# Rows of 320 instead of 272 columns for the operands of the feed-forward matmuls

## The reference

```python
D_FF = 2816

def rms_norm(x, gain):
    x32 = x.astype(jnp.float32)
    y = x32 * lax.rsqrt(jnp.mean(x32 * x32, axis=-1, keepdims=True) + EPS)
    return (y * gain.astype(jnp.float32)).astype(x.dtype)

def swiglu_ffn(h, w_in, w_out):
    gate, up = jnp.split(h @ w_in, 2, axis=-1)
    return (jax.nn.silu(gate) * up) @ w_out

for layer in range(2):
    h = h + 0.5 * swiglu_ffn(rms_norm(h, ffn_norm[layer, 0]), ffn_w_in[layer, 0], ffn_w_out[layer, 0])
    h = h + mixer(layer, rms_norm(h, mix_norm[layer]))
    h = h + 0.5 * swiglu_ffn(rms_norm(h, ffn_norm[layer, 1]), ffn_w_in[layer, 1], ffn_w_out[layer, 1])
return rms_norm(h, final_norm)[:, 16:]
```

## Time and profile before

| what | before |
|---|---|
| median of three runs | 1885.46 us (1885.03 to 1889.59) |
| profiled execution: span, first to last instruction | 1880.4 us |
| mean granted TensorE clock | 0.991 of full |
| TensorE busy | 1814.7 us, 97% |
| weight loads busy (beside the matmuls) | 1734.8 us, 92% |
| VectorE busy | 1282.0 us, 68% |
| ScalarE busy | 1037.5 us, 55% |
| matmuls | 18074 |
| HBM read | 274.96 MB, 147 GB/s over the span |

### The profile page before, as it was taken

The page is one execution under the profiler, slowest core; times in us unless marked ns, Lnnn a source line. Parts: engine busy times, 40 slices in busy tenths (PEclk is TensorE's granted clock), DMA queues, the critical chain, the costliest instruction groups (busy, mean ns, idle before and its releaser), DMA issues.

```text
span 1880.4 us, 46612 instructions
## 1 busy us (share of the span) xinstructions
PE 1814.7 (97%) x18074; PEld 1734.8 (92%) x18074; DVE 1282.0 (68%) x2615; ACT 1037.5 (55%) x2048; POOL 25.6 (1%) x20
## 2 busy tenths in 40 slices
PE   7999999999999999999999999999989988899998
PEld 7999999999999999988899999999987877799998
DVE  6788687678686665586566664666567786657754
ACT  7656656656655554555456554555455744355553
POOL 0110000110000000000000000000000000000000
PEclk9999999999999999999999999999999999999999
DMA  7455566445564555533135555565552320036553
GB/s 252 145 168 179 161 194 181 141 148 162 160 191 136 178 174 173 167 104 95 63 104 165 170 177 176 161 178 169 177 193 90 107 75 4 4 113 190 181 187 123
DMA packets 75966, 278.08 MB, mean 148 GB/s; under 512 B 8497, under 2 KB 9905, under 8 KB 75313
## 3 DMA queue, kind: packets, MB, share of 16 engines
q1 hardware_dynamic: 75824, 276.05, 47.6%
HBM read 274.96 MB, written 1.05 MB: 147 GB/s over the span
## 4 chain that ended last, share of the span: by engine, by line
PE 82%; DVE 10%; ACT 4%; issue 2%; DMA 1%; SPq 0%; DVEq 0%; ACTq 0%
PE psum L414 23%; PE psum L416 23%; PE psum L415 22%; DVE weights_low L379 3%; ACT weights_high L371 2%; PE psum L2932 1%; DMA weight_ring<-weights_in 1%; PE psum L2564 1%; PE psum L1139 1%; PE psum L725 1%; PE psum L2909 1%; PE psum L746 1%; PE psum L554 1%; PE psum L2926 1%; DVE normed L1549 1%
## 5 line engine op out<-in xcount | busy, mean ns | idle before, releaser
L379 DVE TENSOR_TENSOR weights_low<-weight_ring,weights_high 128x512 fp32r<-128x512 f32 x984 | 664.7, 694 | 442.3 <-ACT weights_high L371 431.3
L371 ACT ACTIVATE weights_high<-weight_ring 128x512 fp32r<-128x512 f32 x984 | 607.5, 628 | 539.3 <-PE psum L416 537.9
L414 PE MATMUL psum<-ffn_normed_high,weights_high 128*128 128x272 f32 (+1 forms) x1408 | 406.2, 289 | 4.0 <-DVE weights_low L379 2.6
L416 PE MATMUL psum<-ffn_normed_high,weights_low 128*128 128x272 f32 (+1 forms) x1408 | 404.5, 287 | 0.0
L415 PE MATMUL psum<-ffn_normed_low,weights_high 128*128 128x272 f32 (+1 forms) x1408 | 403.1, 286 | 0.0
L414 PE MATMUL psum<-first_normed_high,weights_high 128*128 128x256 f32 x1024 | 295.6, 289 | 2.9 <-DVE weights_low L379 2.1
L415 PE MATMUL psum<-first_normed_low,weights_high 128*128 128x256 f32 x1024 | 284.5, 278 | 0.0
L416 PE MATMUL psum<-first_normed_high,weights_low 128*128 128x256 f32 x1024 | 284.5, 278 | 0.0
L414 PEld LDWEIGHTS psum<-ffn_normed_high,weights_high 128*128 128x128 f32 x1408 | 265.2, 188 | 7.1 <-issue 6.9
L415 PEld LDWEIGHTS psum<-ffn_normed_low,weights_high 128*128 128x128 f32 x1408 | 265.1, 188 | 0.1
L416 PEld LDWEIGHTS psum<-ffn_normed_high,weights_low 128*128 128x128 f32 x1408 | 265.3, 188 | 0.0
(11 more groups left out here) (467 smaller groups left out, 3114.4 us busy)
## 6 DMA issues: line engine op xcount, KB each, us to landing
weight_ring<-weights_in SPq DMA_DIRECT2D x507, 512.0 KB, 3.6
arena<-first_in SPq DMA_DIRECT2D x1, 2176.0 KB, 10.1
consts<-const_in SPq DMA_DIRECT2D x1, 1895.0 KB, 7.5
arena<-vec_in SPq DMA_DIRECT2D x1, 1536.0 KB, 10.2
arena<-vec_in SPq DMA_DIRECT2D x1, 1152.0 KB, 5.7
residual<-x_in SPq DMA_DIRECT2D x2, 544.0 KB, 4.8
out<-normed SPq DMA_DIRECT2D x4, 256.0 KB, 2.4
weight_ring<-weights_in SPq DMA_DIRECT2D x2, 256.0 KB, 5.0
```

Source lines behind the costliest of these rows:

```text
L371: nc.scalar.activation(WH[:, n % SPLIT, half], W[:, n % RING, half], ACT.Copy).then_inc(weights_high, 1)
L379: nc.vector.tensor_tensor(WL[:, n % SPLIT, half], W[:, n % RING, half], WH[:, n % SPLIT, half].bitcast(F32), ALU.subtract).then_inc(weight ...
L414: nc.tensor.matmul(psum, WH[:, s, cols], high, start=start, stop=False)
L416: return nc.tensor.matmul(psum, WL[:, s, cols], high, start=False, stop=stop)
```

## The change

Feed-forward layers 0 to 2 keep `ffn_normed` and `ffn_inner` in rows of 320 columns (1280 bytes), of which 272 are used. The last layer has tensors of its own names with rows of 272 as before. `ffn_normed` still begins at column 28288 of the arena, so its low part begins 2560 columns further instead of 2176; `ffn_inner` begins at column 0 instead of 4352, in the last layer too; the gate and product buffers follow at 14080 instead of 16320. `pe_ffn`, `act_ffn` and `dve_ffn` take the pair that belongs to their layer. Every instruction, its size, its order and its waits are the same.

```diff
-        H2_H, H2_L = parts("ffn_normed", 13 * KC * S2, KC, S2)
-        F_H, F_L = parts("ffn_inner", 2 * KC * S2, FF_CH, S2)
-        FFN_GATE, FFN_PROD = (arena((2 * KC + 2 * FF_CH + 2 * j) * S2, 2, S2) for j in range(2))
+        FFN_ROW = 320
+        FFN_NORMED = [parts("ffn_normed", 13 * KC * S2, KC, FFN_ROW)] * 3 + [parts("last_normed", 13 * KC * S2, KC, S2)]
+        FFN_INNER = [parts("ffn_inner", 0, FF_CH, FFN_ROW)] * 3 + [parts("last_inner", 0, FF_CH, S2)]
+        FFN_GATE, FFN_PROD = (arena(2 * FF_CH * FFN_ROW + 2 * j * S2, 2, S2) for j in range(2))
...
         def pe_ffn(pe, use, l, f, norm, n=S2):
             block, _ = BLOCKS[f"ffn_in{f}", l]
+            (H2_H, H2_L), (F_H, F_L) = FFN_NORMED[use], FFN_INNER[use]
...
         def act_ffn(act, use, l, f, norm, x, n, first):
             block, _ = BLOCKS[f"ffn_in{f}", l]
+            (H2_H, H2_L), (F_H, F_L) = FFN_NORMED[use], FFN_INNER[use]
...
         def dve_ffn(dve, use, l, f, norm, x, n, add, first):
             block, _ = BLOCKS[f"ffn_in{f}", l]
+            (H2_H, H2_L), (F_H, F_L) = FFN_NORMED[use], FFN_INNER[use]
```

## The result

| | before | changed |
|---|---|---|
| median of five runs | 1886.58 us (1885.03 to 1889.59) | 1877.96 us (1872.08 to 1879.88) |
| span of the profiled execution | 1880.4 us | 1876.2 us, time 1877.96 us |
| three 272-token layers, from the first matmul of each stage to the end of its last, summed | 608.2 us | 597.7 us |
| last feed-forward layer, the same | 191.4 us | 191.4 us |
| matmuls' mean duration, normed input, line 416 | 289 ns | 287 ns |

The changed kernel takes 0.9948 of the time before (95% interval 0.9934 to 0.9962), 7 to 12 us less. The forecast was 1863 us in 1857 to 1888: the side was right, the size 2.6 times too large (22.5 us against 8.6).

What follows compares the result with a forecast made beforehand. TensorE's three matmul lines were taken as the bound. Savings of 18.4 us (normed) and 6.7 us (inner), 25.1 us, less 2.6 us for stage beginnings, left 22.5 us: from 1885.5 to 1863 us, range 1857 to 1888.

Steps and rivals of the forecast that it cites:

- TensorE's three lines are the path, nothing else moves, VectorE and the weights keep up: Whole kernel: 68% of the wait chain runs through lines 414 to 416; VectorE's 4.5 us per two blocks is covered by 5.8.
- Two rates of the same 256-column matmul, by how the stream was entered: 256-column stages: 113.3 or 117.5 ns between starts, kept until an interruption, not set by the place of the data.
- Price of a 272-column matmul in aligned rows ... I take 120.4: Layers 0 to 2: 113.3 ns plus 6.3 to 7.9 for 16 more columns, 119.6 to 121.2 ns, taken as 120.4.
- normed (126.2 - 120.4) x 3168 = 18.4 us: Normed input, layers 0 to 2: 3168 matmuls fall from 126.2 to 120.4 ns, saving 18.4 us.
- inner 6.7 us: Inner product, layers 0 to 2: 1584 matmuls fall from 124.6 to 120.4 ns, saving 6.7 us.
- The 2.6 us for stage beginnings at the long rate: First 4 of 44 normed and 3 of 22 inner blocks, interrupted, gain nothing: 1.7 + 0.9 us off the saving.
- rival A: Layers 0 to 2: aligned rows settle at the long rate, 124.6 ns, 1880 us; chance 0.12, another 0.12 for part of the stages.
- the recorded 287 ns: Recorded duration on lines 414 to 416, 272 columns: 287 would mean the long rate everywhere; about 283 was forecast.
- Even k start at multiples of 128 bytes: Normed input before: even k take 0.37 us, odd k, 64 bytes past such a multiple, 0.38 to 0.39; all rows would be aligned.
- rival C: Layers 0 to 2: the common row start has the dearest relation to the weights, 130 ns a matmul, 1906 us; chance 0.14.
- The 5.1 us between the profiled span and the median: Whole kernel before: median 1885.5 us against span 1880.4, put down to what surrounds the span and added to the forecast span.
- Rival B: Layers 0 to 2: where rows start does not matter, so no effect, 289 ns recorded and 1885.5 us; chance 0.14.

## Why the prediction was right and wrong

- *TensorE's three lines are the path, nothing else moves, VectorE and the weights keep up:* right. The waits on weights stayed under a microsecond in 113 us, and the gain of each stage is its matmuls' and adds up.
- *Two rates of the same 256-column matmul, by how the stream was entered:* right that there are two, shown in isolation too, 113.3 and 117.8 ns; what at the entry picks one is open.
- *"Price of a 272-column matmul in aligned rows ... I take 120.4":* this term failed. It took the price of 16 columns from rows 1088 apart (6.3 to 7.9 ns), where neither width had its best rate, and put it on the best rate of 256 columns. At the good relation the 16 columns cost 10.0 ns (113.3 to 123.3): 256 columns stand 1.6 ns above the floor of 111.7, and the first 4 columns more already cost 6.7. Mis-sized terms: normed (126.2 - 120.4) x 3168 = 18.4 us, measured 2.8 ns a matmul and 8.3 us; inner 6.7 us, measured 1.7 ns (its blocks average 125.0, not the 124.6 of the one I read) and 2.2 us.
- *The 2.6 us for stage beginnings at the long rate:* the share was right, a tenth of the gain, and the reason wrong. At the full step the stages would have gained 2.8 x 3168 = 8.9 and 1.7 x 1584 = 2.7 us; they gained 8.3 and 2.2, so their interrupted blocks kept back 1.1 of 11.6 us. But no long rate is seen in them: in the real kernel 272 columns at this relation have one rate in all six stages (of the isolated groups one had another, 126.7). That is also why rival A, whose 1880 us came nearest, is not what happened: its 124.6 ns was seen in no stage of the changed kernel, although the recorded 287 ns is what the prediction had named as its sign.
- *"Even k start at multiples of 128 bytes", hence cheap, and so will all rows be:* the reading of the trace was right and the reason wrong. The cheap even k held rows at 128 and rows at 0, and once all rows are alike those at 0 are 3.4 ns dearer: a triple's time among mixed rows doesn't tell what its relation costs alone. The change was faster because it put the rows 192 past the weights' remainder; I never looked at where the weights were, though rival C named them.
- *The measured difference* of 8.6 us (7 to 12) holds the 10.5 us of the stages. The 5.1 us between the profiled span and the median were put down to what surrounds a span; the recorded runs have 1.8 us there (1885.03 us with a span of 1883.2, 1877.96 with 1876.2), and the other 3.3 us were scatter of that one execution.
- *Rival B, that places don't matter,* falls: with TensorE alone at work the rate depends on the place of the moving row relative to the weights. The Trainium skill, "SBUF — State Buffer", section "Who interferes with whom", which has TensorE's two read ports as independent and TensorE as never waiting on anyone, is borne out in one half: with all other engines idle the rates are those of the real kernel to 0.3 ns. The independence of the two ports is not: the places of the row and of the weights together decide between 123.3 and 126.7 ns, so the two reads are not independent in what they cost.
- Of places tried none gave 272 columns less than 123.3 ns. The Trainium skill, "TensorE: Matmul & The Clock Gate", section "Wait — 56ns, not 53.3ns?", would give an estimate of 115.8 ns, columns over the clock and its fixed part; the lowest measured for 272 columns, 123.3, is 7.5 ns above it.

## What to carry to other kernels

Where the two-part fp32r matmuls alternate with weight loads, the start distance depends on where the moving row lies relative to the weight tile. Keep the distance between rows (and between high and low) a multiple of 256 bytes, so that it is one relation and not four in turn, and then measure a few offsets of 64 bytes in a kernel of TensorE alone, at the width that will be used (a difference of 64 reaches the short rate at 256 columns and is the dearest at 272): it gave the real kernel's rates to 0.3 ns, in one run. A wrong common offset is worse than none: 612 us against 608 for mixed rows and 598 for the good one. And price a width by its own measurement, never by the slope of another layout.

## What the runs showed that I had not expected

- A floor of 111.7 ns per fp32r matmul with its own weights, for 128, 192 and 224 columns alike; 256 columns cost 1.6 ns more, 260 cost 8.3 ns more.
- The relation of row and weights, modulo 256 bytes, worth 3.4 ns at 272 columns and up to 6.7 ns at 256 (113.3 against 120.0), with other good differences at one width than at the other.
- Eight bytes matter: 123.3 ns at a difference of 192, 126.7 at 184 and 200. What in the memory makes it so stays open.
- Two rates for 256 columns, held over hundreds of matmuls and changed only by an interruption; the same code came out at 276 or 281 ns in different executions (branch products: 4.2 ns x 576 starts, 2.4 us), which is one source of the scatter between runs.
